# One step of a two-layer decoder trunk: where the next head's queries are split inside the attention loop

## The reference, cut to what matters

```python
s = einsum('bqhc,bkc->bhqk', ql, c) + einsum('bqhr,bkr->bhqk', qr, kr)
s = s * ks[:, :, None, :] * scale
s = where(k_pos <= q_pos, s, NEG_INF)
p = softmax(s, axis=-1)
o = einsum('bhqk,bkc->bqhc', p, c)                    # latent output of a head
o = einsum('bshc,chv->bshv', o, w_uv); y = o @ w_o    # values, output projection
```

## Time and profile before

| | |
|---|---|
| median of 3 runs | 2070.93 us (2070.41 to 2072.74) |
| the profiled execution | 2071.63 us, of which the span of instructions 2069.2 us |
| TensorE busy in the span | 2045.8 us (99%) |
| VectorE, ScalarE, GpSimd busy | 1611.0, 1127.6, 364.1 us |
| granted TensorE clock, mean | 0.998 of full speed |
| attention over heads | from about 1509 to 1676 us, with the 46 us of the output projection inside |

### The profile page before, as it was taken

The page is one execution under the profiler, slowest core; times in us unless marked ns, Lnnn a source line. Parts: engine busy times, 40 slices in busy tenths (PEclk is TensorE's granted clock), DMA queues, the critical chain, the costliest instruction groups (busy, mean ns, idle before and its releaser), DMA issues.

```text
span 2069.2 us, 44545 instructions
## 1 busy us (share of the span) xinstructions
PE 2045.8 (99%) x16756; PEld 1996.9 (97%) x16756; DVE 1611.0 (78%) x2687; ACT 1127.6 (54%) x1956; POOL 364.1 (18%) x437
## 2 busy tenths in 40 slices
PE   9999999999999999999999999999999999999999
PEld 8999999999999999999999999998779899999998
DVE  6779885426366998988899898669676578989997
ACT  5446554433134665655665565446585556656555
POOL 0011111122011111111111111112232221111111
PEclk9999999999999999999999999999999999999999
DMA  5467783232314777776677777443322227777775
GB/s 161 120 160 180 185 194 119 82 102 62 103 62 126 173 183 182 183 175 161 157 179 188 182 181 183 123 136 98 94 77 77 62 68 159 180 184 177 185 184 130
DMA packets 362556, 295.71 MB, mean 143 GB/s; under 512 B 22103, under 2 KB 327556, under 8 KB 362148
## 3 DMA queue, kind: packets, MB, share of 16 engines
q1 hardware_dynamic: 325498, 227.26, 37.0%
q0 software_dynamic: 36592, 66.07, 19.3%
q10 hardware_dynamic: 314, 0.37, 0.1%
HBM read 224.57 MB, written 2.66 MB: 110 GB/s over the span
## 4 chain that ended last, share of the span: by engine, by line
PE 87%; DVE 5%; DMA 3%; ACT 2%; issue 2%; POOL 1%; SPq 0%; ACTq 0%; DVEq 0%
PE side L859 29%; PE main L810 25%; PE main L859 21%; PE side L1413 1%; DMA raw<-raw 1%; PE main L1162 1%; DMA raw<-in_ffn_w_gate 1%; PE side L1250 1%; DVE w_lo L2182 1%; PE side L1078 1%; PE main L1230 1%; DMA sums_w<-raw 1%; PE main L1330 1%; PE main L1315 1%; PE main L1422 1%
## 5 line engine op out<-in xcount | busy, mean ns | idle before, releaser
L859 PE MATMUL side<-xw_hi,w_hi 128*128 128x260 f32 x1344 | 380.9, 283 | 5.0 <-DVE tmp_in L2331 2.1
L859 PE MATMUL side<-xw_hi,w_lo 128*128 128x260 f32 x1344 | 381.0, 284 | 0.0
L859 PE MATMUL side<-xw_lo,w_hi 128*128 128x260 f32 x1344 | 380.1, 283 | 0.0
L2182 DVE TENSOR_TENSOR w_lo<-raw,w_hi 128x512 fp32r<-128x512 f32 (+2 forms) x472 | 323.4, 685 | 39.0 <-ACT w_hi L1540 20.5
L859 PE MATMUL main<-xw_hi,w_hi 128*128 128x260 f32 x1008 | 286.1, 284 | 0.0
L859 PE MATMUL main<-xw_lo,w_hi 128*128 128x260 f32 x1008 | 284.7, 282 | 0.0
L859 PE MATMUL main<-xw_hi,w_lo 128*128 128x260 f32 x1008 | 284.5, 282 | 0.0
L859 PEld LDWEIGHTS side<-xw_hi,w_hi 128*128 128x128 f32 x1344 | 253.2, 188 | 8.0 <-DVE tmp_in L2331 3.5
L859 PEld LDWEIGHTS side<-xw_hi,w_lo 128*128 128x128 f32 x1344 | 253.1, 188 | 0.0
L859 PEld LDWEIGHTS side<-xw_lo,w_hi 128*128 128x128 f32 x1344 | 252.8, 188 | 0.0
L3126 POOL DMA_DIRECT2D sums_w<-raw x116 | 100.8, 869 | 700.2 <-DMA raw<-in_ffn_w_gate 325.7
(11 more groups left out here) (471 smaller groups left out, 5440.3 us busy)
## 6 DMA issues: line engine op xcount, KB each, us to landing
sums_w<-raw POOLq DMA_DIRECT2D x112, 256.0 KB, 3.3
raw<-raw POOLq DMA_DIRECT2D x112, 256.0 KB, 5.1
raw<-in_ffn_w_gate SPq DMA_DIRECT2D x86, 256.0 KB, 4.5
raw<-in_ffn_w_gate SPq DMA_DIRECT2D x43, 512.0 KB, 6.0
raw<-in_ffn_w_up SPq DMA_DIRECT2D x84, 256.0 KB, 4.2
raw<-in_ffn_w_up SPq DMA_DIRECT2D x42, 512.0 KB, 6.2
raw<-in_gmlp_w_in SPq DMA_DIRECT2D x16, 1024.0 KB, 5.5
raw<-in_ffn_w_down SPq DMA_DIRECT2D x56, 256.0 KB, 4.0
```

The source lines that it names most:

```text
L859: mm = nc.tensor.matmul(into[j], w_tiles(w, weights_at(s, j))[:, k, :], moving[:, k, order[j], :], start=(j in (0, 1) and k == 0 and i == ...
L2182: a = nc.vector.tensor_tensor(dst, src, hi.bitcast(F32), ALU.subtract)
```

## The change

In steps 1 to 13 without step 9, ScalarE rounds the queries of head h + 2 right behind the exponentials of head h, and the high half of the values moves behind that of the output. On GpSimd in the same steps the low half of those queries comes before the wait for `prob_done` instead of after it and after the low half of the values. In all steps the two small instructions on the sample's outputs move behind the projection's piece and the low half of the value weights. No instruction is added or taken away, and the lists of TensorE, VectorE and the transfers stay as they are.

```diff
@@ scalar, in the loop over h, behind the exponentials
+                queries_first = 1 <= h < H - 2 and h != KC + 1
+                if queries_first:
+                    split_queries(h + 2)
                 def head_hi(f):
                     act.wait_ge(uv_copied, f + 1)
                     nc.scalar.activation(h_hi[:, f % KC, :], square[:, f % 2, :], ACT.Copy).then_inc(h_hi_done, 1)
 
-                if g >= 1:
+                if g >= 1 and not queries_first:
                     head_hi(g - 1)
                 if g >= 0:
                     act.wait_ge(pv_done, g + 1)
                     nc.scalar.activation(o_hi[:, 0:SEQ], side[:, 2, :], ACT.Copy).then_inc(head_hi_set, 1)
+                if g >= 1 and queries_first:
+                    head_hi(g - 1)
...
                 if h + 2 < H:
                     move_rope(h + 2)
-                    split_queries(h + 2)
+                    if not queries_first:
+                        split_queries(h + 2)
@@ gpsimd, in the loop over h
-                if h >= 1:
-                    if h >= 2:
-                        pool.wait_ge(uv_done, h - 1)
-                    o_sample = o_s[:, :].rearrange("p (b h) -> p b h", h=H)[:, :, h - 1]
-                    nc.gpsimd.tensor_copy(o_hi[:, SEQ:TOK], o_sample).then_inc(o_samples, 1)
-                    pool.wait_ge(o_samples, 2 * h - 1)
-                    nc.gpsimd.tensor_tensor(o_lo[:, SEQ:TOK], o_sample, o_hi[:, SEQ:TOK].bitcast(F32),
-                                            ALU.subtract).then_inc(o_samples, 1)
                 if h < H:
                     pool.wait_ge(max_done, h + 1)
...
                     nc.gpsimd.tensor_tensor(uv_lo[:, h - 1, :], wkv[:, h - 1, :], uv_hi[:, (h - 1) % 2, :].bitcast(F32),
                                             ALU.subtract).then_inc(kv_lo_set, 1)
+                if h >= 1:
+                    if h >= 2:
+                        pool.wait_ge(uv_done, h - 1)
+                    o_sample = o_s[:, :].rearrange("p (b h) -> p b h", h=H)[:, :, h - 1]
+                    nc.gpsimd.tensor_copy(o_hi[:, SEQ:TOK], o_sample).then_inc(o_samples, 1)
+                    pool.wait_ge(o_samples, 2 * h - 1)
+                    nc.gpsimd.tensor_tensor(o_lo[:, SEQ:TOK], o_sample, o_hi[:, SEQ:TOK].bitcast(F32),
+                                            ALU.subtract).then_inc(o_samples, 1)
+                queries_first = 1 <= h < H - 2 and h != KC + 1
+                if queries_first:
+                    query_rest(h + 2)
                 if h < H and h != KC + 1:
                     pool.wait_ge(prob_done, h + 1)
                 if h >= 2:
                     value_rest(h - 2)
-                if h + 2 < H:
+                if h + 2 < H and not queries_first:
                     query_rest(h + 2)
```

## The result

The changed kernel takes 2072.82 us (median of 20 runs), the kernel before, run beside it, 2069.46: a ratio of 1.0018, 95% interval 1.0012 to 1.0024, or +3.7 us (2.5 to 5.0). It is slower, and by less than 0.2% in the middle of the interval. The profiled execution took 2073.32 us with a span of 2071.4, 2.2 over the span before.

The account below looks back on a forecast made before the run. TensorE, busy 99% of the span, bounds the kernel; with the scaling blocked, the VectorE - ScalarE loop sets the pace at 7.97 us. +2.65 and +1.50 give +4.15 us, median 2070.93 to 2075.1, range 2071.5 to 2076.8.

Parts of the forecast that it names:

- All waits for `q_lo` go: TensorE's latent products: `q_lo` ends over 2 us before its use, so four matmul and nine weight-load waits vanish.
- ScalarE's reordering costs nothing: ScalarE behind the exponentials: `q_hi` and `head_hi` swap places at zero cost, at most 0.63 us a step if not covered.
- The block, 1.07 us in twelve steps: VectorE's four scalings: `q_lo` on GpSimd beside them delays them 1.07 us in steps 1 to 8 and 10 to 13.
- the shorter block: Rival, chance 0.14: scaling to L3091 takes 2.10 us instead of 2.26, the loop 7.81, together +2.2 us, 2073.1.
- The loop, 7.97 us: Loop VectorE - ScalarE - VectorE, once per head: 6.90 us unblocked, 7.97 blocked, 0.47 a step slower than TensorE's 7.50.
- +2.65 and +1.50 us: Delay of the attention loop's first part (to head 9) and second part (to head 15), summing to +4.15 us.
- the full block: Main case, chance 0.70: the scaling loses 1.07 us in each of 12 steps, range +3.2 to +5.2 us.
- Half on either side of 0.2%: Whole kernel: the sum lies on the 0.2% (4.14 us) edge, half of the main case's 0.70 on either side.
- TensorE idle 0.4 to 0.5 us a step, the projection 2.6 us later: Changed profile: TensorE idles before the transposes L1372, waiting for the scaling; the output projection's first product comes about 2.6 us later.
- The next four steps, with pieces: Attention loop from 1539.07: four steps with GpSimd's projection pieces take 31.81 us, 7.95 a step, TensorE idle for 1.55.
- TensorE's own pace of 7.50: Attention loop: three steps take 22.51 us with TensorE busy throughout, so 7.50 us a step is its own work.
- the rival in which GpSimd waits: Rival, chance 0.14: `q_lo` runs behind the four scalings; four steps go from 7.95 to 7.50, 1.8 us won, 2069.0.

Follow-up runs that it names:

- e4: The kernel before with only ScalarE's part of the change, GpSimd's order left as before; one run, 2077.45 us, span 2074.8.
- e1: The changed kernel with GpSimd taking the queries' low half after the wait for `prob_done`, ahead of the values' low half; 2067.33 us against 2070.95 before, ratio 0.9982.
- e3: The changed kernel with one more 128x512 GpSimd subtraction right ahead of the queries' low half in the same 12 steps; one run, 2086.37 us.
- e8: The kernel before with GpSimd alone changed: pieces behind the maximum, queries' low half ahead of the values' behind `prob_done`; 2070.27 us against 2069.35, ratio 1.0010.

## Why the prediction was right, point by point

- *All waits for `q_lo` go.* Right but for one load that waits 0.3 us for the `q_lo` of step 0, which the change leaves alone. Before, nine loads and four matmuls waited.
- *ScalarE's reordering costs nothing.* Right in the changed kernel. e4 shows that the cover is GpSimd's new order, which I had not said: with the old one it costs 3.1 us.
- *The block, 1.07 us in twelve steps.* Right in mechanism and steps. L3093 takes 2.29 to 2.31 us, so the block is 1.03. L3097 starts 2.22 after it, where I took 2.26 from step 9. By the step alone the shorter block, my rival with 7.81, would fit as well as the full one with 7.97. This distance decides: 2.22 against 2.10 and 2.26.
- *The loop, 7.97 us.* Measured 7.89. The block was 0.04 over. From L3056 to L3093 it is 5.07 where step 1 before had 5.09. From L3097 to L3056 it is 0.60 in all these steps, where I had taken the middle of 0.60 and 0.65; the 0.65 came from a step in which a piece ran.
- *+2.65 and +1.50 us.* Measured +2.00 and +1.17, the same 0.08 us in each of the twelve blocked steps. This is the term that was mis-sized. The sum of +4.15 became +3.2 in the trace, at the low end of the +3.2 to +5.2 that I gave the full block, and +3.7 (2.5 to 5.0) in the runs.
- *Half on either side of 0.2%.* The middle, 0.18%, lies just within, and the interval (0.12% to 0.24%) lies on both sides; on which side the middle fell is luck. The kernel took 2072.8 where I had forecast 2075.1, of which 1.5 is the kernel before itself, which came out at 2069.5 in the new runs.
- *TensorE idle 0.4 to 0.5 us a step, the projection 2.6 us later.* The matmul rows show 0.3 idle a step, half before the first transpose and half before the third. The projection's first product comes at 1577.99, before at 1575.28. The 2.71 us look like the forecast, but 0.71 of them is the later start of the stage; the change made 2.00.
- *The next four steps, with pieces.* A slip in reading: the row from 1539.07 covers steps 5 to 8, and the pieces run in steps 4 to 7. The sum of the forecast did not use it.
- *TensorE's own pace of 7.50.* Wrong, though the sum did not hang on it. I read three steps with TensorE busy throughout as its floor. e1 shows 7.31: the ends of matmuls are modelled, and a wait of 0.18 us in the weight loads leaves no gap in them. Where even the loads show no wait, the starts give it away. Step 3 of the kernel before, GpSimd's `q_lo` and then TensorE's first transpose and first latent product:

```profile
1523.94 1.29 POOL L3244 TENSOR_TENSOR q_lo<-qn,q_hi 128x512 fp32r<-128x512 f32 x1
...
1524.08 1.31 PE L1372 MATMUL side<-const,prob 128*128 128x128 f32 x10
1525.29 0.33 PE L1315 MATMUL main<-c_hi,q_hi 128*128 128x128 f32 x1
```

The product starts 0.06 us after `q_lo` ends and 1.21 us after the first transpose; in e1 that second distance is 1.06 to 1.07 in every step from 2 to 8. So most steps of the kernel before waited for `q_lo` as well, and the rival in which GpSimd waits would have given about 4.1 us instead of 1.9, as e1 did. In e1 the marks are 57.88 and 31.35 us apart, 3.2 and 0.8 less than before.

## What to carry to other kernels

Before a GpSimd instruction is moved, list what VectorE runs beside it. Two kinds stood still here until the GpSimd instruction was done: one that moves two columns a nanosecond (a float32 tensor_scalar from SBUF to SBUF), and one with two inputs in SBUF, though it was four columns wide. What one is moved *behind* can be worth more than what it is moved ahead of: with everything else as changed, the attention costs 3 us more than before with the low half beside the scaling and 4 less with it behind. The loop here closes 0.45 us under TensorE's pace, and so it hid nearly all of a block of 0.48 and not one of 1.03. Sum the loop before placing work beside it.

## What the runs showed of the hardware that I had not expected

- GpSimd gets in between two VectorE instructions of one run of four, and does so twice in a row: with two of its instructions queued, the third scaling took 1.44 us and the fourth 1.48 (e3, step 5; unblocked they take 0.41 and 0.48).
- A VectorE instruction of four columns took 1.00 us instead of 0.15 beside a GpSimd subtraction (e8).
- Full busy time of TensorE over 22 us hid up to 0.2 us a step of waiting for `q_lo`; in some steps no row shows the wait, and only the starts do.
